# First feed-forward of a two-layer backbone: x times scale into the up-products, the root multiplied in behind them

## The chip, the cores and the metric

The kernel runs on one core of a Trainium2 chip. The metric is the device time of one execution in microseconds; the kernel before has a median of 1995.95 us over 3 runs.

## The reference, cut to what matters

The model has two layers over 512 latent tokens and 256 context tokens with 1024 features. Layer 0 is retention and a gated ConvFFN, layer 1 neighbourhood attention and a gated ConvFFN on the latents. The change is in layer 0, between the retention's output projection and the feed-forward.

```python
def _rmsnorm(x, w):
    y = xf * lax.rsqrt(jnp.mean(xf * xf, axis=-1, keepdims=True) + NORM_EPS)
    return (y * w).astype(x.dtype)

x = x + g1 * y
h2 = _rmsnorm(x, norm2_w) * (1 + sc2) + sh2
x = x + g2 * _conv_ffn(h2, w_up, conv_w, conv_b, w_down)

def _conv_ffn(h, w_up, conv_w, conv_b, w_down):
    u = h @ w_up                       # 1024 -> 2 x 2816
    u = conv over 3 neighbouring tokens, per feature, zeros outside, + conv_b
    a, g = jnp.split(u, 2, axis=-1)
    return (jax.nn.silu(a) * g) @ w_down
```

The scale and the shift are one value per feature and condition (latent, context); the root is one value per token.

## The kernel before, in words

Features lie on the 128 partitions, tokens along the free dimension; x is 8 chunks of 128 features by 768 tokens (512 latent, then 256 context). Each product is done with both operands split in a rounded part (`_hi`) and the rest (`_lo`), as three matmuls: `w_hi` with `h_hi`, `w_hi` with `h_lo`, `w_lo` with `h_hi` (`product`, L404), each once for 512 and once for 256 columns. A block in this document is one chunk of 128 input features in one such product: 6 matmuls. `project` is 8 blocks into one accumulator of two banks; two accumulators take turns, and TensorE waits for `acc_taken` before it opens one again.

Weights come as 512 KB chunks on SP's queue into two `raw` buffers. ScalarE copies each to `w_hi` (L873), VectorE computes `w_lo` (L1304) and counts `lo_split`, which TensorE waits for and which lets SP load the next chunk. There are two slots for split chunks and a spare one.

The order on each engine is the order in the code, with semaphores between engines. In the retention's last output projection (`out_projection`, final) each of 8 tiles m has 4 blocks. VectorE adds it into x (`add_gated`, L1476), ScalarE squares x (L915, the last in two parts, L923 and L925), and VectorE adds the square to `ss` (L1329). Then `final_sums` on TensorE sums over features with matmuls against ones (L480 the sum so far, L488 the last square), ScalarE takes the root (L903), VectorE its reciprocal (L1335), and `spread_roots` brings it to all partitions (L455). TensorE fills the waits with `keep_busy` matmuls (L471). The norm then makes h chunk by chunk: VectorE x times scale times root (L1451), ScalarE plus shift, rounded, into `h_hi` (L955), VectorE the rest into `h_lo` (L1460). `project_two` (L503) does the first two up-products block by block in step with this.

The feed-forward takes its 22 pairs of feature blocks in groups of 8, 8 and 6: for each pair two projects (ups), and after each group 8 tiles down into x. The first two down tiles are interleaved (`outputs_start`, L662), with the last block of each behind the others. For each pair `inner` runs on ScalarE and VectorE: ScalarE evicts the accumulator into `u` (L1074) with pad columns that are zero, VectorE does the three taps (L1665, L1666, L1668), ScalarE Silu (L1080), VectorE the product (L1677), ScalarE `act_hi` (L1085), VectorE `act_lo` (L1685). In between VectorE computes the modulation for layer 1 from rows that POOL's queue loads (`ada_step`, L1416 and L1418): for two conditions in the first group, for one later.

## Time and profile before

| | |
|---|---|
| runs | 1997.66, 1995.95, 1995.14 us |
| profiled execution | 1995.96 us |
| its span | 1993.9 us |
| TensorE matmuls | 1964.6 us busy |
| VectorE | 1288.7 us busy |
| ScalarE | 717.5 us busy |
| GpSimd | 93.0 us busy |

The span is what the profiler records between first and last instruction; the execution's own time lies around it. Times of rows are microseconds from the start of the span unless marked ns. A matmul in plain fp32 (L455, L480, L488) is recorded as two. Some matmul records are missing, so counts can fall short by a few. In a list by line, the columns are line, engine, operation, output<-inputs, shapes and count, then total busy us and mean ns of one, then idle time before. In a list in order of time they are start, duration, engine, line, operation, and in brackets the idle time before and what ended it.

### The profile page before, as it was taken

The page shows a single profiled execution, that of the slowest core. Times are in us where ns is not written, and L with a number is a line of the kernel's source. Part 1 is how long each engine was busy: PE and PEld are TensorE (multiplying, and loading weights), DVE is VectorE, ACT ScalarE, POOL GpSimd, SP SyncE. Part 2 cuts the span into 40 slices and gives each one's busy share as a digit, 9 for nine tenths or more (in the row PEclk, how much of TensorE's full clock was granted, in tenths as well). Part 3 has the DMA queues.
Part 4 walks back from the last instruction along what each step waited for, and adds up shares of the span by engine and source line. Part 5 has one row for each costly group of instructions (what it writes and reads, how often), then busy time and mean ns, then how long its engine had stood idle before and what let it go on. Part 6 is the DMA issues. An engine that isn't in the chain of part 4 may idle for free.

```text
span 1993.9 us, 29041 instructions
## 1 busy us (share of the span) xinstructions
PE 1964.6 (99%) x10628; PEld 1684.8 (84%) x10628; DVE 1288.7 (65%) x1976; ACT 717.5 (36%) x1111; POOL 93.0 (5%) x161
## 2 busy tenths in 40 slices
PE   8999999999999999999999999999999999999998
PEld 8888888888888888888888888788888778888886
DVE  7865645735645677765665467867777777467376
ACT  5433224223313343312331233355665543233243
POOL 0000000000000000000000000211111000000000
PEclk9999999999999999999999999999999999999999
DMA  7321311321222112233223323321111322233223
GB/s 307 99 88 64 106 64 54 106 71 57 85 95 64 54 64 95 95 121 115 94 94 125 116 95 127 121 98 55 53 49 48 106 85 95 95 95 103 86 95 106
DMA packets 51268, 186.56 MB, mean 94 GB/s; under 512 B 5680, under 2 KB 5680, under 8 KB 51184
## 3 DMA queue, kind: packets, MB, share of 16 engines
q1 hardware_dynamic: 37744, 136.73, 20.8%
q0 software_dynamic: 13440, 48.63, 7.4%
q8 instruction: 62, 1.02, 0.2%
q14 instruction: 22, 0.18, 0.0%
HBM read 181.15 MB, written 4.19 MB: 93 GB/s over the span
## 4 chain that ended last, share of the span: by engine, by line
PE 94%; DVE 2%; ACT 1%; DMA 1%; issue 1%; SPq 0%; DVEq 0%; ACTq 0%; POOLq 0%
PE acc L404 60%; PE acc L722 6%; PE o_ps L541 4%; PE acc L662 4%; PE o_ps L572 3%; PE acc L541 3%; PE o_ps L722 2%; PE acc L559 2%; PE acc L503 2%; PE acc L757 1%; PE o_ps L708 1%; PE o_ps L687 1%; PE acc L695 1%; DMA ada_start<-in_ada_first_dram 1%; PE o_ps L455 1%
## 5 line engine op out<-in xcount | busy, mean ns | idle before, releaser
L873 ACT ACTIVATE w_hi<-raw 128x1024 fp32r<-128x1024 f32 x223 | 235.8, 1057 | 582.8 <-PE acc L404 466.8
L404 PE MATMUL acc<-h_hi,w_hi 128*128 128x512 f32 x1520 | 434.2, 349 | 3.5 <-ACT u L1074 1.8
L1304 DVE TENSOR_TENSOR w_lo<-raw,w_hi 128x1024 fp32r<-128x1024 f32 x223 | 272.8, 1223 | 252.4 <-ACT w_hi L873 250.8
L404 PE MATMUL acc<-h_lo,w_hi 128*128 128x512 f32 x1520 | 434.8, 349 | 0.0
L404 PE MATMUL acc<-h_hi,w_lo 128*128 128x512 f32 x1520 | 433.7, 348 | 0.0
L404 PEld LDWEIGHTS acc<-h_hi,w_hi 128*128 128x128 f32 x1520 | 243.6, 188 | 43.4 <-ACT u L1074 2.6
L404 PEld LDWEIGHTS acc<-h_hi,w_lo 128*128 128x128 f32 x1520 | 244.5, 188 | 39.3
L404 PEld LDWEIGHTS acc<-h_lo,w_hi 128*128 128x128 f32 x1520 | 243.6, 188 | 38.2
L1476 DVE SCALAR_TENSOR_TENSOR x<-acc,mod,x 128x512 f32<-128x512 f32 (+3 forms) x137 | 82.0, 634 | 149.5 <-PE acc L404 120.0
L404 PE MATMUL acc<-act_hi,w_hi 128*128 128x512 f32 (+1 forms) x396 | 119.9, 356 | 1.3 <-DVE x L1476 1.3
L404 PE MATMUL acc<-act_hi,w_lo 128*128 128x512 f32 (+1 forms) x396 | 120.2, 357 | 0.0
L404 PE MATMUL acc<-act_lo,w_hi 128*128 128x512 f32 (+1 forms) x396 | 119.5, 355 | 0.0
L1418 DVE CUSTOM_DVE_ANT_0 ada_raw<-ada_raw,silu_rows 128x1024 f32<-128x1024 f32 x80 | 97.8, 1223 | 7.5 <-DMA ada_raw<-in_ada_dram 5.7
L321 POOL DMA_DIRECT2D ada_raw<-in_ada_dram x79 | 41.8, 529 | 1164.7 <-DVE mod_new L1418 1164.7
L1085 ACT ACTIVATE act_hi<-scratch 128x768 f32 (+3 forms) x44 | 32.6, 740 | 141.3 <-DVE scratch L1677 141.3
L1666 DVE SCALAR_TENSOR_TENSOR scratch<-u,taps,scratch 128x769 f32<-128x769 f32 (+1 forms) x88 | 78.1, 887 | 3.1
L1668 DVE SCALAR_TENSOR_TENSOR scratch<-u,taps,scratch 128x769 f32<-128x769 f32 (+1 forms) x88 | 78.0, 887 | 3.1
L404 PEld LDWEIGHTS acc<-act_hi,w_hi 128*128 128x128 f32 x396 | 65.1, 187 | 15.1 <-DVE x L1476 3.5
L404 PEld LDWEIGHTS acc<-act_lo,w_hi 128*128 128x128 f32 x396 | 65.1, 188 | 12.1
L404 PEld LDWEIGHTS acc<-act_hi,w_lo 128*128 128x128 f32 x396 | 65.1, 187 | 11.6
L1074 ACT ACTIVATE u<-acc 128x512 f32<-128x512 f32 (+1 forms) x132 | 62.9, 514 | 24.5 <-PE acc L404 24.5
L1172 ACT ACTIVATE pt_hi<-acc 128x512 fp32r<-128x512 f32 x64 | 38.3, 599 | 84.2 <-PE acc L695 84.1
(263 smaller groups left out, 3385.3 us busy)
## 6 DMA issues: line engine op xcount, KB each, us to landing
raw<-in_weights_dram SPq DMA_DIRECT2D x232, 512.0 KB, 3.4
ada_raw<-in_ada_dram POOLq DMA_DIRECT2D x80, 512.0 KB, 3.8
ada_start<-in_ada_first_dram SPq DMA_DIRECT2D x8, 1024.0 KB, 19.9
x<-in_x_in_dram SPq DMA_DIRECT2D x4, 768.0 KB, 7.4
park_dram<-x POOLq DMA_DIRECT2D x1, 2048.0 KB, 8.1
rel<-in_bias_dram POOLq DMA_DIRECT2D x16, 128.0 KB, 2.4
x<-park_dram POOLq DMA_DIRECT2D x2, 1024.0 KB, 6.6
out_dram<-x SPq DMA_DIRECT2D x8, 256.0 KB, 2.2
```

The lines of the kernel that those rows point to most:

```text
L404: mm = nc.tensor.matmul(tile[:, c0:c0 + cn], wt[:, b * P:(b + 1) * P], mv[:, n, c0:c0 + cn], start=(n == 0 and m == 0), stop=(n == last an ...
L541: mm = nc.tensor.matmul(tile, hs[:, k, t * P:(t + 1) * P], ws[:, d * RV:(d + 1) * RV], start=(k == 0 and m == 0), stop=(last and m == 2))
L572: mm = nc.tensor.matmul(tile, vt[:, c0:c0 + P], pt[i % 2][:, p0:p0 + qn], start=((context or i == 0) and n == 0 and m == 0), stop=(i >= 5 ...
L662: mm = nc.tensor.matmul(tile[:, c0:c0 + cn], wt[:, n * P:(n + 1) * P], mv[:, n, c0:c0 + cn], start=(n == 0 and m == 0), stop=(n == size - ...
L722: mm = nc.tensor.matmul(tile[:, c0:c0 + cn], wt[:, n * P:(n + 1) * P], mv[:, n, c0:c0 + cn], start=(n == 0 and m == 0), stop=(n == KC - 1 ...
L873: nc.scalar.activation(w_hi[i][:, :] if spare is None else spare[0], raw[r][:, :], ACT.Copy).then_inc(hi_split, 1)
L1074: ins = nc.scalar.activation(u[j][:, c0 + c + 1:c0 + c + 1 + cn], tile[:, c0:c0 + cn], ACT.Copy)
L1304: nc.vector.tensor_tensor(lo, raw[r][:, :], hi.bitcast(F32), ALU.subtract).then_inc(lo_split, 1)
L1418: nc.vector.tensor_tensor_reduce(ada_raw[:, :], ada_raw[:, :], silu_rows[:, 0, :], 1.0, 0.0, ALU.mult, ALU.add, mod_new[:, j, 0:1]).then_i ...
L1476: ins = nc.vector.scalar_tensor_tensor(xv, tile[:, c0:c0 + cn], mod[:, layer, bass.ds(gate + m, 1), c:c + 1].rearrange("p a c -> p (a c)") ...
L1666: step(nc.vector.scalar_tensor_tensor(S[j][:, 0:width], u[j][:, 1:1 + width], tap(1), S[j][:, 0:width], ALU.mult, ALU.add))
L1668: nc.vector.scalar_tensor_tensor(S[j][:, 0:width], u[j][:, 2:2 + width], tap(2), S[j][:, 0:width], ALU.mult, ALU.add).then_inc(conv_done, 1)
```

## The change

The scale is made before the output projection (`lift_scale`). As each chunk of x is complete, ScalarE and VectorE write x times scale, without the root and the shift, into `h_hi` and `h_lo` (`scaled_hi`, `scaled_lo`). Two columns behind the 768 hold the shift for the latents and for the context, so the row of `h_hi` and `h_lo` is 770 long and the second matmul of each up-product has 258 columns (`WITH_SHIFT`). The norm and the double product are gone in this place; two ordinary projects stand there, and the sums of squares (`sums_so_far`, `last_sums`, the two halves of `final_sums`) and `spread_roots` stand before blocks 3, 4 and 6 of the first. ScalarE copies the spread roots into `ss`. VectorE, and no longer ScalarE, evicts each up-product, times `ss`, into `u`. The shift's product is constant along the tokens: it goes times the sum of the taps into the bias (`lifted`), and the pads of `u` hold its negative; each part now has pads of its own. The first tap is done by ScalarE and no longer by VectorE. Layer 1 keeps its order. `lift` now shares its place with `cond`, and POOL's two waits on `norm_t` count 8 less, for the norm that is gone.

```diff
-        h_hi = sb("h_hi", [P, KC, TOK], F32R)
-        h_lo = sb("h_lo", [P, KC, TOK], F32R)
+        h_hi = sb("h_hi", [P, KC, TOK + 2], F32R)
+        h_lo = sb("h_lo", [P, KC, TOK + 2], F32R)
...
+                def ready_and_chain(n):
+                    ready(n)
+                    if n in chain:
+                        chain[n]()
...
+                        if chain is None:
+                            project_two(ups, ready, spare)
+                        else:
+                            project(h_hi, h_lo, ups, ready_and_chain)
+                            project(h_hi, h_lo, ups, None, spare)
...
             out_projection(True)
-            final_sums(TOK)
-            keep_busy(2)
-            spread_roots(PARTS, True)
-            keep_busy(12)
-            ffn(PARTS, spare1)
+            ffn(WITH_SHIFT, PARTS, spare1, {3: lambda: sums_so_far(TOK), 4: lambda: last_sums(TOK), 6: lambda: spread_roots(PARTS)})
...
+            def scaled_hi(k):
+                for c0, cn, c in PARTS:
+                    ins = nc.scalar.activation(h_hi[:, k, c0:c0 + cn], x[:, k, c0:c0 + cn], ACT.Identity, scale=norm_a[:, k, c:c + 1])
+                ins.then_inc(h_hi_done, 1)
+            def copy_spread():
+                root(D, TOK, True)
+                act.wait_ge(spread_done, roots.now())
+                nc.scalar.activation(ss[:, :], spread[:, 0:TOK], ACT.Copy).then_inc(spread_copied, 1)
...
                         if j < splits:
                             split()
-                        if j == 0:
-                            act.wait_ge(conv_done, convs.now() + (layer + 1))
-                        for c0, cn, c in parts:
-                            ins = nc.scalar.activation(u[j][:, c0 + c + 1:c0 + c + 1 + cn], tile[:, c0:c0 + cn], ACT.Copy)
-                        ins.then_inc(acc_taken[i], 1)
+                        if layer:
+                            if j == 0:
+                                act.wait_ge(conv_done, convs.now() + 1)
+                            nc.scalar.activation(u[j][:, 1:1 + LAT], tile[:, 0:LAT], ACT.Copy).then_inc(acc_taken[i], 1)
+                        else:
+                            act.wait_ge(acc_taken[i], after)
+                            for c0, c1, c in ((0, LAT + 2, 0), (LAT + 2, TOK + 2, 1)):
+                                ins = nc.scalar.activation(S[j][:, c0:c1], u[j][:, c0:c1], ACT.Identity,
+                                                           scale=taps[:, 4 * j:4 * j + 1], bias=lifted[:, j, c:c + 1])
+                            ins.then_inc(conv_begun, 1)
                         if spare is not None and j == 0:
                             split(spare)
-                    act.wait_ge(conv_done, convs.now() + (layer + 2))
...
                         last_square(t, after, TOK)
                     else:
                         final_square(t, after, 2 * c, m, TOK)
+                    if c == 0 and m == 0:
+                        act.wait_ge(scale_made, 1)
+                        nc.scalar.activation(h_hi[:, :, TOK:TOK + 2], mod[:, 0, 24:24 + KC, :], ACT.Copy)
+                    scaled_hi(2 * c + m)
                     if c == OUT_SLOTS - 1 and m == 0:
                         split(spare1)
-            x_final()
-            norm(0, 24, PARTS)
+            copy_spread()
             ffn(0, PARTS, False)
...
+            def scaled_lo(k):
+                dve.wait_ge(h_hi_done, h_hi_made.up())
+                for c0, cn, c in PARTS:
+                    ins = nc.vector.scalar_tensor_tensor(h_lo[:, k, c0:c0 + cn], x[:, k, c0:c0 + cn], norm_a[:, k, c:c + 1],
+                                                         h_hi[:, k, c0:c0 + cn].bitcast(F32), ALU.mult, ALU.subtract)
+                ins.then_inc(h_lo_done, 1)
...
             def out_projection(with_ada, first_ada=0, final=False):
                 if final:
                     step(nc.vector.memset(ss[:, :], 0.0))
+                    lift_scale(0, 2, 24, 2).then_inc(scale_made, 1)
                 own_done()
                 for m in range(KC):
                     add_gated(m, 0, 16, PARTS, final and m == KC - 1)
...
                     if final and m < KC - 1:
                         add_square(m % 2, TOK)
+                    if final:
+                        scaled_lo(m)
+                    if final and m == 0:
+                        nc.vector.tensor_tensor(h_lo[:, :, TOK:TOK + 2], mod[:, 0, 24:24 + KC, :],
+                                                h_hi[:, :, TOK:TOK + 2].bitcast(F32), ALU.subtract)
                     if final and m == KC - 2:
                         split(spare1)
...
                 if final:
                     squares_made.up()
+                    h_split.up(KC)
+                    one_over(TOK)
+                    dve.wait_ge(spread_copied, 2)
...
                     conds = 2 if n == 0 else 1
                     ups = UP_ADA[n] if with_ada else 0
                     steps = [(hi_splits, 2), (own_steps, 5 + ups * conds), (silus, 1), (act_hi_made, 1)]
-                    steps += [(ada_loads, 16 * ups), (ada_made, ups)]
+                    steps += [(ada_loads, 16 * ups), (ada_made, ups), (begun, 0 if layer else 2)]
                     def inner(f, splits, spare=None):
-                        step(nc.vector.tensor_copy(taps[:, :], conv[:, layer, bass.ds(f + f0, 1), :].rearrange("p a c -> p (a c)")))
+                        step(nc.vector.tensor_copy(taps[:, 0:8], conv[:, layer, bass.ds(f + f0, 1), :].rearrange("p a c -> p (a c)")))
+                        if not layer:
+                            own = lambda t: taps[:, 0:8].rearrange("p (j t) -> p t j", t=4)[:, t, :]
+                            step(nc.vector.tensor_tensor(taps[:, 8:10], own(0), own(1), ALU.add))
+                            step(nc.vector.tensor_tensor(taps[:, 8:10], taps[:, 8:10], own(2), ALU.add))
                         for j in range(2):
                             i, _, _, after = A.next()
                             dve.wait_ge(acc_full, A.full.now())
+                            tap = lambda t: taps[:, 4 * j + t:4 * j + t + 1]
+                            if not layer:
+                                tile = acc[i]
+                                nc.vector.scalar_tensor_tensor(lifted[:, j, :], tile[:, TOK:TOK + 2], taps[:, 8 + j:9 + j],
+                                                               tap(3).to_broadcast([P, 2]), ALU.mult, ALU.add)
+                                for c, ends in ((0, slice(0, LAT + 2, LAT + 1)), (1, slice(LAT + 2, TOK + 4, CTX + 1))):
+                                    nc.vector.tensor_scalar(u[j][:, ends], tile[:, TOK + c:TOK + c + 1].to_broadcast([P, 2]), -1.0, None,
+                                                            ALU.mult)
+                                for c0, cn, c in parts:
+                                    at = c0 + 2 * c + 1
+                                    ins = nc.vector.tensor_tensor(u[j][:, at:at + cn], tile[:, c0:c0 + cn], ss[:, c0:c0 + cn], ALU.mult)
+                                ins.then_inc(acc_taken[i], 1)
                             if j < splits:
                                 split()
-                            dve.wait_ge(acc_taken[i], after)
-                            tap = lambda t: taps[:, 4 * j + t:4 * j + t + 1]
-                            step(nc.vector.tensor_scalar(S[j][:, 0:width], u[j][:, 0:width], tap(0), tap(3), ALU.mult, ALU.add))
+                            if layer:
+                                dve.wait_ge(acc_taken[i], after)
+                                step(nc.vector.tensor_scalar(S[j][:, 0:width], u[j][:, 0:width], tap(0), tap(3), ALU.mult, ALU.add))
+                            else:
+                                dve.wait_ge(conv_begun, begun.up())
                             step(nc.vector.scalar_tensor_tensor(S[j][:, 0:width], u[j][:, 1:1 + width], tap(1), S[j][:, 0:width],
...
                         for c0, cn, c in parts:
-                            ins = nc.vector.tensor_tensor(S[3][:, c0:c0 + cn], S[2][:, c0 + c:c0 + c + cn],
-                                                          S[1][:, c0 + c:c0 + c + cn], ALU.mult)
+                            own = slice(c0 + 2 * c, c0 + 2 * c + cn)
+                            ins = nc.vector.tensor_tensor(S[3][:, c0:c0 + cn], S[2][:, own], S[1][:, own], ALU.mult)
...
             out_projection(0, final=True)
-            pads()
-            norm(0, 2, 24, PARTS, False)
             ffn(0, PARTS, True, False)
```

## Rows read from the trace of the kernel before

**Rows 1.** The page: engines, and the chain that ended last by engine.
```profile
PE 1964.6 (99%) x10628; PEld 1684.8 (84%) x10628; DVE 1288.7 (65%) x1976; ACT 717.5 (36%) x1111; POOL 93.0 (5%) x161
...
PE 94%; DVE 2%; ACT 1%; DMA 1%; issue 1%; SPq 0%; DVEq 0%; ACTq 0%; POOLq 0%
```

**Rows 2.** The chain in order of time: start, duration, what; longest pieces.
```profile
677.83 25.48 PE acc L404 x144
...
712.40 16.76 PE acc L503 x90
...
731.05 118.99 PE acc L404 x672
850.04 15.72 PE acc L662 x90
...
866.98 183.79 PE acc L404 x1056
```

**Rows 3.** The chain again, 665 to 765 us, with its short pieces.
```profile
703.31 1.28 PE o_ps L480 x12
...
705.58 1.30 PE o_ps L488 x12
...
707.51 1.17 PE o_ps L455 x8
...
729.18 1.06 ACT w_hi L873
730.24 0.77 ACT u L1074 x2
```

**Rows 4.** Busy by engine in stretches: length, PE, PEld, DVE, ACT, POOL, PEclk, DMA.
```profile
703.30:712.40 9.10, 8.45 (x56) 7.02 (x54) 6.20 (x19) 4.50 (x10) 0.00 (x0) 1.00 0.35 115
...
731.00:850.00 119.00, 118.95 (x673) 103.13 (x674) 91.50 (x126) 37.07 (x63) 3.70 (x7) 1.00 0.29 95
```

**Rows 5.** In order of time, 690 to 735 us: one chunk of the norm.
```profile
713.34 1.14 DVE L1460 SCALAR_TENSOR_TENSOR h_lo<-scratch,mod,h_hi 128x512 fp32r<-128x512 f32 x2
713.46 1.13 ACT L955 ACTIVATE h_hi<-scratch,mod 128x512 fp32r<-128x512 f32 x2 [1.41 <-DVE scratch L1451]
```

**Rows 6.** In order of time, 665 to 700 us: the first tiles' adds.
```profile
676.54 1.14 DVE L1476 SCALAR_TENSOR_TENSOR x<-acc,mod,x 128x512 f32<-128x512 f32 x2 [0.75 <-PE acc L618]
...
677.77 0.84 ACT L915 ACTIVATE scratch<-x 128x768 f32<-128x768 f32 x1 [3.77 <-DVE x L1476]
...
678.65 0.96 DVE L1329 TENSOR_TENSOR ss<-ss,scratch 128x768 f32<-128x768 f32 x1 [0.96 <-ACT scratch L915]
...
679.52 1.14 DVE L1476 SCALAR_TENSOR_TENSOR x<-acc,mod,x 128x512 f32<-128x512 f32 x2
```

**Rows 7.** ScalarE in order of time, 703 to 760 us.
```profile
702.18 1.28 ACT L896 ACT_TABLE_LOAD   x1
...
703.59 1.04 ACT L873 ACTIVATE w_hi<-raw 128x1024 fp32r<-128x1024 f32 x1
704.54 0.61 ACT L923 ACTIVATE scratch<-x 128x512 f32<-128x512 f32 x1
```

**Rows 8.** VectorE by line and shape, 15 to 90 us.
```profile
L1533 DVE TENSOR_TENSOR vg_lo<-acc,vg_hi 128x512 fp32r<-128x512 f32 x4 | 2.6, 686 | 3.1 <-ACT vg_hi L983 3.1
...
L1356 DVE TENSOR_SCALAR norm_a<-mod_new,lift,small 128x2 f32<-128x2 f32 x8 | 2.3, 288 | 0.3
...
L1515 DVE TENSOR_TENSOR qk_lo<-acc,qk_hi 128x256 fp32r<-128x256 f32 x1 | 0.4, 425 | 0.0
```

**Rows 9.** VectorE by line and shape, 660 to 850 us.
```profile
L1665 DVE TENSOR_SCALAR scratch<-u,taps 128x769 f32<-128x769 f32 x15 | 10.2, 678 | 0.0
```

**Rows 10.** ScalarE in order of time, 0 to 30 us.
```profile
25.86 1.31 ACT L939 ACTIVATE scratch<-scratch,mod,norm_a 128x512 f32<-128x512 f32 x2 [1.10 <-DVE scratch L1373]
```

**Rows 11.** VectorE in order of time, 800 to 870 us.
```profile
856.10 0.95 DVE L1685 TENSOR_TENSOR act_lo<-scratch,act_hi 128x768 fp32r<-128x768 f32 x1
```

**Rows 12.** The page: one of the costliest groups.
```profile
L404 PE MATMUL acc<-h_hi,w_hi 128*128 128x512 f32 x1520 | 434.2, 349 | 3.5 <-ACT u L1074 1.8
```

More of the change, by code:

```diff
@@ L61 @@
 PARTS = ((0, LAT, 0), (LAT, CTX, 1))
+WITH_SHIFT = ((0, LAT, 0), (LAT, CTX + 2, 1))
 WIDE = 64
@@ L203, in backbone @@
                 u = [sb(f"u{i}", [P, TOK + 4], stack=part) for i in range(2)]
-                taps = sb("taps", [P, 8], stack=part)
+                taps = sb("taps", [P, 10], stack=part)
+                lifted = sb("lifted", [P, 2, 2], stack=part)
                 waste = sb("waste", [P, D], stack=part)
@@ L406, in product, with project @@
                 mm.then_inc(acc_full, 1)
-            def project(hi, lo, parts, ready=None):
-                w = next_chunk()
+            def project(hi, lo, parts, ready=None, spare=None):
+                w = next_chunk(spare)
                 product(open_acc(), w, range(KC), hi, lo, parts, ready)
@@ L471, in keep_busy, with sums_so_far @@
                     nc.tensor.matmul(o_ps[:, 2, :] if place is None else place, w[:, 0:P], w[:, 0:LAT], start=True, stop=True)
-            def final_sums(width, ends=False):
-                if not ends:
-                    pe.wait_ge(lo_split, chunk.now() + 1)
-                half = LAT if width == TOK else LAT // 2
+            def sums_so_far(width):
                 pe.wait_ge(sq_added, squares_added.up(KC) - 1)
@@ L490, in final_sums @@
                 mm.then_inc(sums_done, 1)
+            def final_sums(width, ends=False):
+                if not ends:
+                    pe.wait_ge(lo_split, chunk.now() + 1)
+                sums_so_far(width)
+                keep_busy(4)
+                last_sums(width)
             def project_two(parts, ready, spare, tiles=None):
@@ L626, in out_projection, with ffn @@
                         product(open_acc(), w, range(m * VC, (m + 1) * VC), hi, lo, PARTS)
-            def ffn(parts, spare):
+            def ffn(ups, downs, spare, chain=None):
                 ready = h_ready(h_split.now())
                 first = True
+                def ready_and_chain(n):
+                    ready(n)
+                    if n in chain:
+                        chain[n]()
                 for size in GROUPS:
@@ L638, in ffn @@
                         h_split.up(KC)
-                        project_two(parts, ready, spare)
+                        if chain is None:
[3 more added lines that the diff above has]
+                            project(h_hi, h_lo, ups, None, spare)
                     with turns(pe, size - first, A.steps(2) + [(chunk, 2)]):
-                        project(h_hi, h_lo, parts)
-                        project(h_hi, h_lo, parts)
+                        project(h_hi, h_lo, ups)
+                        project(h_hi, h_lo, ups)
                     first = False
                     act_split.up(size)
-                    outputs_start(size, parts, act_ready, spare)
+                    outputs_start(size, downs, act_ready, spare)
                     with turns(pe, 3, A.steps(2) + [(chunk, 2)]):
@@ L648, in ffn @@
                             w = next_chunk()
-                            product(open_acc(), w, range(size), act_hi, act_lo, parts)
+                            product(open_acc(), w, range(size), act_hi, act_lo, downs)
             def outputs_start(size, parts, ready, spare):
@@ L1432, in norm @@
                 own_done()
-                step(nc.vector.scalar_tensor_tensor(
-                    norm_a[:, :, 0:n], mod[:, layer, shift + KC:shift + 2 * KC, 0:n], 1.0,
-                    norm_w[:, which, :].rearrange("p (k c) -> p k c", c=1).to_broadcast([P, KC, n]), ALU.add, ALU.mult))
+                step(lift_scale(layer, which, shift, n))
                 one_over(width)
@@ L1481, in add_gated, with lift_scale @@
                 ins.then_inc(acc_taken[i], 1)
+            def lift_scale(layer, which, shift, n):
+                return nc.vector.scalar_tensor_tensor(
+                    norm_a[:, :, 0:n], mod[:, layer, shift + KC:shift + 2 * KC, 0:n], 1.0,
+                    norm_w[:, which, :].rearrange("p (k c) -> p k c", c=1).to_broadcast([P, KC, n]), ALU.add, ALU.mult)
+            def scaled_lo(k):
[4 more added lines that the diff above has]
+                ins.then_inc(h_lo_done, 1)
             def out_projection(with_ada, first_ada=0, final=False):
```

33 lines of the change are left out of this document (19 added, 14 removed).

## The prediction

> **What bounds the kernel now.** I read the engine shares first, then the chain that ended last, and then went closer only where the change works. TensorE is busy 99% of the span and makes up 94% of the chain [rows 1]: time is won only where TensorE stands idle or does work that nothing needs. The chain shows one such place in reach: out-projection tiles run from 677.83 for 25.48 us, the double first product of the feed-forward starts only at 712.40, and the plain run of up-products only at 731.05 [rows 2]. Between them stand the norm (sums of squares 1.28 and 1.30, spread of the roots 1.17, the rest waiting for ScalarE and VectorE) and, after the double product, a gap in which a weight split (1.06) and an eviction (0.77) come first [rows 3]. So 703.31 to 731.05, 27.74 us, is the stretch to watch. The granted clock there is 1.00, the 2.4 GHz level [rows 4]; it is not what costs.
>
> **A block of product.** A project is 8 blocks of 6 matmuls. 14 projects took 118.99 us for 672 matmuls: 0.1771 us each, 1.06 us a block, 8.50 a project. The later ups and downs took 183.79 for 1056, that is 0.1740 each or 1.04 to 1.05 a block [rows 2]. Out-projection tiles have 4 blocks: 25.2 us for 6 tiles, 4.20 each.
>
> **Part 1: the stretch.** Taken out of it: the wait for roots, the first scaled h, and the waiting gap at its end. Left on TensorE: 16 blocks at 1.06 = 16.96 us, plus the three small groups now between the blocks: 1.28 + 1.30 and, for the whole spread of which the chain shows the first 8 of 12 matmuls (1.17), 1.3. Sum 20.8 us. Against 27.74 this frees 6.9 us if nothing waits. Now what waits:
>
> **Part 2: out-projection on ScalarE and VectorE.** Per tile ScalarE adds scaled_hi (like L955, 1.13 us for the two parts) and VectorE scaled_lo (like L1460, 1.14) [rows 5]. VectorE works in order: the add of tile m at G, ScalarE's square from G+1.23 to G+2.07 [rows 6], scaled_hi to about G+3.1, VectorE's add of the square from G+2.1, scaled_lo from G+3.15, next add at G+4.2. The weight split of the odd tiles falls into the wait for the square. The cycle is thus 4.2 us, just the 4.20 of a tile: VectorE keeps pace but has no reserve. It starts late: behind tile 0 stand scaled_lo(0), the two shift columns and their ScalarE copy (about 0.1 to 0.2 each on either engine, like other operations on a few columns), so the add of tile 1 moves from 679.52 [rows 6] to 681.0. It frees its accumulator at 682.1, and TensorE, done with tile 2 at 682.03, waits 0.25 us. Each later add ends within 0.05 us of TensorE's need. Cost: 0.25 us; lower bound 0; upper bound, if each of six cycles runs as much over as the first, 6 x 0.25 = 1.5.
>
> **Part 3: the last tile.** Add 6 starts at 702.0 and TensorE starts the first project at 703.56. ScalarE then does square 6, scaled_hi(6), the split into the spare (from 705.0), the table load (1.28) and its dummy, a split (1.04), and only then the half squares [rows 7]. With the same spacing they come at 708.5 to 709.4 and scaled_hi(7) ends at 710.4, so scaled_lo(7) ends at 711.6. TensorE: blocks 0 to 2 end at 706.7, sums so far at 708.0, block 3 at 709.1, and the half square is there at 709.2. The wait for it has all further blocks queued behind it; I take 0.1 us, bounds 0 and 2 (ScalarE's list half as long again). The reciprocal, behind scaled_lo(7) on VectorE, is ready at 711.7 and the spread is asked for at 712.6, after block 5: hidden with 0.9 us to spare. Block 7 needs scaled_lo(7): hidden by 3 us. The accumulator is full at 716.1; ScalarE's copy of the spread (0.8) is done at 715.1 and its Silu table (1.28) loads beside the eviction. The second project runs to 724.7, the first tile is taken near 717.7, so the third project starts without a wait at 724.7 and not at 731.05. **Gain 6.35 us.** The weight loads on SP's queue follow the splits that move later by about 5 us, and land long before the split at 716; no DMA is added. POOL's waits get smaller counts for the same later event: nothing.
>
> **Part 4: the up loop.** VectorE was busy 91.50 of 119 us, 13.1 us for each of 7 pairs (a pair of projects, one pass of the loop, is 16.96) [rows 4]. Taken out: two first taps of 0.68 [rows 9]. Added twice: the eviction (0.69 + 0.43, 1.03 with overlap, [rows 8]), the lifted columns (0.29, [rows 8]) and two pads of 0.1 to 0.2; once: two sums of taps. 13.1 - 1.4 + 2.1 + 1.1 + 0.4 = 15.3 us of 16.96. ScalarE swaps an eviction for a tap with two pointer operands (1.31 for both parts, [rows 10]). The added wait is VectorE's for that tap: in it 1.3 us pass while VectorE has 1.14 us of split to do; behind it stand the other taps, the ada step and the next eviction. Following the order through, a pair needs about 16.6 us in the first group and 1.2 less later, where the ada step has one condition. TensorE waits only when an eviction comes some 6 us late, or the last act_lo: before it ended 7.0 us after the last project of a group [rows 2, 11], now about 8.2; it is wanted after 10 blocks, 10.5 us, in the group of six and after 14 elsewhere. Cost 0, hidden by the other tile's project; upper bound 1 us a pair over pace, of which the 6 us of reserve swallow all but 1 us in the first group.
>
> **Part 5: two columns.** 352 blocks have 3 matmuls that grow from 256 to 258 columns, 1056 in all. 2 columns at 2.4 GHz are 0.83 ns: 0.9 us. Unknown is how TensorE takes 258 columns and rows of h at 770 instead of 768 elements; no row shows either. The nearest rows are the blocks themselves, which run at 1.04 to 1.06 us without a cause that I can see: bounds -0.02 us on the first group's 112 blocks (-2.2 us) and +0.02 on the 224 of the later groups (+4.5), which with the 0.9 gives -1.3 and +5.4. I take 0.9, since the columns are the only known change.
>
> The Trainium skill (VectorE: DVE Perf Modes, the section on the TRN2 errata) prices a matmul at 6 cycles plus its columns. By it a pair of 512 and 256 would take 0.325 us, where the rows give 0.348 to 0.354, so the measured time decides for the fixed part; for two more columns the rule gives 0.83 ns too, and the estimate for this part would stay 0.9 us. What it speaks against is any step in the cost above 256 columns.
>
> **Sum.** 1995.96 us (the profiled execution; span 1993.9 and 2.1 around it; the median of the runs is 0.01 away) - 6.35 + 0.9 = 1990.5. With the 0.2 us on the middle of part 2's and 3's bounds I say **1990.7**.
>
> **Rivals.**
> A, the in-order chain. VectorE has no reserve in the out-projection; if each cycle is 4.45 us and the last square comes late, 1.5 + 1.0 us are lost: 1993.2. For it: 4.2 against 4.20. Against it: the split's overlap was seen in the rows, and the first project needs only six finished blocks at once.
> B, the slower side: rows of h at a stride of 3080 bytes. If this holds TensorE up, it does so in every product with h, in the retention and the second layer as well. 1520 matmuls of one kind [rows 12], less 336 in the second layer's ups, are 592 two-part blocks; at +0.02 us each 11.8 us: 2002.5. From 0.009 us a block on, all gain is gone. For it: blocks of equal work do differ by 0.02 us. Against it: the slow ones and the fast ones share the same stride now.
> C, the first group's blocks fall from 1.06 to 1.04: 2.2 us more gain, 1988.5. For it: every later group does so [rows 2]. Against it: the same instructions kept 1.06 for 119 us.
> D, VectorE sets the pace of the up loop, as the work moved onto it is slower than planned (1 us over pace in all 7, 8 and 6 pairs, of which the reserve swallows 6 us a group): 1, 2 and 0 us, and act_lo of the last group 3.7 us late: 1997.4. For it: 15.3 of 16.96 us. Against it: the adds all come from rows of like shape.
>
> **Chances.** Forecast 0.52 (own range 1989.2 to 1992.2), A 0.15, B 0.13, C 0.13, D 0.07. Faster by over 0.2% (4.0 us, about what a measurement of this kernel can tell from no change) means below 1992.0: 0.48 of the forecast, C, a little of A: 0.62. Slower by that much: most of B and a bit of D, 0.10. The rest 0.28. The range, 1987.8 to 1998, takes in C, A, D and a mild B.
>
> **What would show it.** Right: in the chain no norm between the out-projection and the up-products; the first up-product within 0.5 us of 703.5; sums and spread between its blocks; the third project near 724.7; VectorE 15 to 15.5 us busy a pair, with TensorE never waiting for an eviction. Wrong: TensorE waiting on x or on the half square over 1 us (A); blocks with h over 1.07 us, also in the retention (B); a wait on evictions or act_lo in the loop (D).

## The result: 0.5% slower

The changed kernel takes 2004.57 us (median of 5 runs, 2003.50 to 2005.77) against 1995.14 (1994.28 to 1997.66) for the kernel before (5 runs): a ratio of 1.0046, 95% interval 1.0035 to 1.0056. Forecast was 1990.7, with 1987.8 to 1998.0 as range. The profiled execution took 2004.57, its span 2002.7 (1993.9 before).

The page of the changed kernel, engines and chain; they answer to [rows 1]:
```profile
PE 1975.4 (99%) x10610; PEld 1688.9 (84%) x10610; DVE 1313.2 (66%) x2173; ACT 741.8 (37%) x1113; POOL 93.2 (5%) x161
...
PE 94%; DVE 2%; DMA 1%; ACT 1%; issue 1%; SPq 0%; DVEq 0%; POOLq 0%; ACTq 0%
```
TensorE has 18 matmul records fewer and is busy 10.8 us longer, at a granted clock of 0.998 (0.997 before). So the loss lies in the matmuls themselves, neither in a wait nor in the clock. The chain says where (start, duration, what):
```profile
70.21 42.29 PE acc L406 x240
...
157.31 81.53 PE acc L406 x462
...
682.43 28.95 PE acc L406 x162
...
718.58 129.84 PE acc L406 x732
848.41 15.83 PE acc L682 x90
865.47 187.46 PE acc L406 x1056
1052.93 15.83 PE acc L682 x90
1069.98 152.70 PE acc L406 x864
1222.68 11.61 PE acc L682 x66
...
1620.90 10.97 PE acc L513 x45
1633.49 78.30 PE acc L406 x336
...
1723.01 122.43 PE acc L406 x528
```
and of the kernel before, the rows of the same view that stand in no group above:
```profile
71.25 42.39 PE acc L404 x240
...
158.33 80.41 PE acc L404 x462
...
1067.73 150.51 PE acc L404 x864
1218.24 11.56 PE acc L662 x66
...
1615.59 10.95 PE acc L503 x45
1628.15 76.46 PE acc L404 x336
...
1715.96 120.95 PE acc L404 x528
```
Take the difference of the starts (after less before) at equal pieces: -1.04 us near 71, +4.60 where the out-projection begins (682.43 against 677.83), -1.63 at the end of the first group's ups (848.41, 850.04), +2.16 before the next downs, +4.44 at 1222, +5.31 at 1620, +8.8 at the end. So the changed stretch and its loop gained 6.23 us, as the prediction wanted, while the retention up to there, whose instructions the change leaves alone, lost 5.64, the later groups 3.79 and 2.28, the attention 0.87 and the second layer 3.49. Equal pieces show it without sums: 462 matmuls 81.53 for 80.41, 336 of the second layer 78.30 for 76.46.

The stretch itself, the chain in short pieces:
```profile
711.38 1.29 PE o_ps L479 x12
712.67 1.11 PE acc L406 x6
713.78 1.28 PE o_ps L490 x12
715.06 2.18 PE acc L406 x12
717.24 1.34 PE o_ps L457 x12
```
Sums, half sums and spread stand between blocks with nothing in between, and behind them 732 matmuls run in one piece: the wait for the roots and the gap of [rows 3] are gone.

### The profile page after: what moved, and what is told of

Read it like the earlier page. It is cut to its first block, busy times and chain, and to the rows that moved or that the text cites. A ratio compares the mean times of both kernels' runs of the same rounds, so it can differ in the third digit from the quotient of the medians.

```text
span 2002.7 us, 29213 instructions
## 1 busy us (share of the span) xinstructions
PE 1975.4 (99%) x10610; PEld 1688.9 (84%) x10610; DVE 1313.2 (66%) x2173; ACT 741.8 (37%) x1113; POOL 93.2 (5%) x161
## 4 chain that ended last, share of the span: by engine, by line
PE 94%; DVE 2%; DMA 1%; ACT 1%; issue 1%; SPq 0%; DVEq 0%; POOLq 0%; ACTq 0%
PE acc L406 62%; PE acc L742 6%; PE o_ps L551 4%; PE acc L682 4%; PE o_ps L582 3%; PE acc L551 3%; PE o_ps L742 2%; PE acc L569 2%; PE acc L777 1%; PE o_ps L728 1%; PE o_ps L707 1%; PE acc L715 1%; PE acc L513 1%; DMA ada_start<-in_ada_first_dram 1%; PE o_ps L457 1%
## 5 line engine op out<-in xcount | busy, mean ns | idle before, releaser
L406 PE MATMUL acc<-h_hi,w_hi 128*128 128x512 f32 (+2 forms) x1536 | 443.0, 352 | 2.6 <-issue 1.7
L406 PE MATMUL acc<-h_lo,w_hi 128*128 128x512 f32 (+2 forms) x1536 | 442.7, 351 | 0.0
L406 PE MATMUL acc<-h_hi,w_lo 128*128 128x512 f32 (+2 forms) x1536 | 441.9, 351 | 0.0
L1342 DVE TENSOR_TENSOR w_lo<-raw,w_hi 128x1024 fp32r<-128x1024 f32 x223 | 272.5, 1222 | 188.7 <-ACT w_hi L889 187.4
L406 PEld LDWEIGHTS acc<-h_hi,w_hi 128*128 128x128 f32 x1536 | 248.6, 189 | 44.8 <-issue 2.3
L406 PEld LDWEIGHTS acc<-h_lo,w_hi 128*128 128x128 f32 x1536 | 248.6, 189 | 42.2
L1744 DVE SCALAR_TENSOR_TENSOR scratch<-u,taps,scratch 128x770 f32<-128x770 f32 (+1 forms) x88 | 78.0, 887 | 17.4 <-ACT scratch L1108 15.9
L1746 DVE SCALAR_TENSOR_TENSOR scratch<-u,taps,scratch 128x770 f32<-128x770 f32 (+1 forms) x88 | 78.0, 887 | 3.1
L1108 ACT ACTIVATE scratch<-u,lifted,taps 128x514 f32<-128x514 f32 x88 | 57.9, 706 | 46.0 <-DVE u L1735 46.0
L406 PEld LDWEIGHTS acc<-act_lo,w_hi 128*128 128x128 f32 x396 | 65.0, 188 | 10.8
```

Source lines behind the costliest of these rows:

```text
L406: mm = nc.tensor.matmul(tile[:, c0:c0 + cn], wt[:, b * P:(b + 1) * P], mv[:, n, c0:c0 + cn], start=(n == 0 and m == 0), stop=(n == last an ...
L1108: ins = nc.scalar.activation(S[j][:, c0:c1], u[j][:, c0:c1], ACT.Identity, scale=taps[:, 4 * j:4 * j + 1], bias=lifted[:, j, c:c + 1])
L1342: nc.vector.tensor_tensor(lo, raw[r][:, :], hi.bitcast(F32), ALU.subtract).then_inc(lo_split, 1)
L1744: step(nc.vector.scalar_tensor_tensor(S[j][:, 0:width], u[j][:, 1:1 + width], tap(1), S[j][:, 0:width], ALU.mult, ALU.add))
L1746: nc.vector.scalar_tensor_tensor(S[j][:, 0:width], u[j][:, 2:2 + width], tap(2), S[j][:, 0:width], ALU.mult, ALU.add).then_inc(conv_done, 1)
```

## The experiments

The question: what slows matmuls that are the same instructions as before? What differs for them is the memory. Rows of h are 3080 bytes long instead of 3072, and behind the two longer tensors everything moved: h_lo by 64 bytes, the weights by 128, all tensors of the stages by 96; among these are vg, the moving operand (the one streamed past the weights) of the output projection, and act, that of the downs. The layout theory says that row length and places alone cost the time. The first rival, mix, says that the added work of VectorE and ScalarE gets in TensorE's way; the second, columns, that the two columns cost far more than 0.83 ns. (The expectations call the layout M in e1, its two halves S, the row length, and B, the places, in e2 and e3, and both rivals together P.) Each ratio is to the kernel before in runs beside it. A piece below is a stretch of the chain.

**e1_layout**: the program before, with the changed kernel's memory (`lift` in the place of `cond` too).
```diff
-        h_hi = sb("h_hi", [P, KC, TOK], F32R)
-        h_lo = sb("h_lo", [P, KC, TOK], F32R)
+        h_hi = sb("h_hi", [P, KC, TOK + 2], F32R)
+        h_lo = sb("h_lo", [P, KC, TOK + 2], F32R)
```


> The program of before with the memory layout of after and nothing else of the change: rows of h_hi and h_lo of 770 elements, lift in the place of cond, so that all tensors behind h lie where after has them. Theory M (memory layout: the stride of h, or the places of the tensors behind it, slows the matmuls): the retention loses the 5.4 us that it lost in after (add of tile 0 at about 681), the later stages some 9 more, 2007 to 2011 us in all. Theory P (the loss belongs to the changed program, its 258 columns or its work on VectorE): 1995 to 1997, add of tile 0 at 676 to 677.

2010.21 us, 1.0070 (1.0053 to 1.0086). The chain of this kernel:
```profile
157.55 81.53 PE acc L403 x462
...
871.73 186.49 PE acc L403 x1056
...
1639.51 78.30 PE acc L403 x336
```
81.53 and 78.30 to the hundredth as in the changed kernel. The layout alone costs 14 us, more than the whole loss; in this layout the change's own work gains about 6 (the span is 2008.8 here, 2002.7 with the change).

**e2_places**: rows of 768 as before, but all tensors where the change put them (64 unused bytes behind h_hi and behind h_lo).

> The program of before, rows of h at 768 elements as before, but 64 bytes left free behind h_hi and behind h_lo and lift in the place of cond: every tensor lies where after has it, only the stride of h is that of before. If the stride alone slows (theory S): 1995 to 1998 us, output projection tiles at 4.20 us. If the places do it (theory B: a start off 64 bytes for the retention's and feed-forward's own tensors): as the first kernel, 2005 us and more, output projection tiles at 4.24 us, since those read no h at all.

2000.92, 1.0028 (1.0018 to 1.0039), between the two forecasts. The places cost about 5 us, the row length, on top of them, the other 9.

**e3_rows784**: the changed program; the changed feed-forward has rows of its own, 784 elements, laid over h and dist; everything else lies at its old remainder.
```diff
+            g_hi = sb("g_hi", [P, KC, ROW], F32R, part)
+            g_lo = sb("g_lo", [P, KC, ROW], F32R, part)
```


> The program of after with h at 768 elements a row everywhere but in the changed feed-forward, which has views of its own with rows of 784 elements (3136 bytes, a multiple of 64) over h and dist; lift as before, so that the tensors behind lie at the same remainder of 64 as before. Theories S and B: the retention is back to the times of before, the gain of the changed stretch stays (6.2 us from the add of tile 0 to the end of the first group's ups) and the total is 1988 to 1991 us. Theory P: no better than 2002.

1992.30, 0.9981 (0.9972 to 0.9991): faster than before, and just above the 1988 to 1991 forecast. Retention and second layer are back (80.41, 76.46); the ups of the later groups still take 186.34 and 152.42 us.

**e4_256cols**: the changed kernel with 256 columns in the second matmul; the product of the shift is left out.
```diff
-WITH_SHIFT = ((0, LAT, 0), (LAT, CTX + 2, 1))
+WITH_SHIFT = PARTS
```


> The program and layout of after with 256 instead of 258 columns in the second matmul of each up-product (the product of the shift is left out, so the output is another). If two columns cost what columns cost: 0.9 us less than after, 2003.7. If 258 crosses a step: 3 to 5 us less, 2000 to 2001.5, with blocks of 1.04 in the groups of 8 and 6. If only the layout matters: 2003 to 2004.

2002.84, 1.0034 (1.0022 to 1.0047). The three up pieces took 129.05, 186.50 and 152.66 us, 1.8 us less than with 258 columns; here the columns explain no more than that.

**e5_784_256cols**, **e6_768_256cols**, **e7_rows800**: e3_rows784 with 256 columns; with 256 columns and rows of 768 (in both the shift's product is left out, in the second its two copies too); with rows of 800 and all of the change.

> The version with rows of 784 for the changed feed-forward, its second matmul of 256 columns instead of 258, so that the product of the shift is left out. Question: in the version with 258 columns the stretches that hold the ups of the second and third group still took 186.3 and 152.4 us against 183.8 and 150.5 in the kernel before. If the two columns cost it: 183.8 and 150.5 come back and the time is about 1988. If the length of the rows costs it (784 as 770): 186 and 152 stay, about 1991.5, the two columns being worth 1 us. If it is the other mix of work on VectorE and ScalarE: the same as for the rows, and the version with rows of 768 tells the two apart.

> The same, with rows of 768 as everywhere before, so without room for the shift columns: neither their two small copies nor their product are made. All else of the change is in. If the row length holds TensorE up: 183.8 and 150.5 us in the two stretches and 1986 to 1988 us, 8 to 10 below the kernel before. If the other mix of work on VectorE and ScalarE slows TensorE in the up loop: 186 and 152 stay and about 1991.

> The version with 784-element rows, with 800 instead (3200 bytes, a multiple of 128 where 3136 is only one of 64), shift and 258 columns in. If only a multiple of 64 counts: as with 784, 1992.3 within 1 us, 186.3 and 152.4 in the two stretches. If a larger power of two counts: below 1991, with 184 to 185.5 and 151 to 152. If what counts is how far 8 rows lie apart in the memory, not their remainder: slower than 784, 1993 to 1994.

e5 1990.13, 0.9972 (0.9962 to 0.9982); e6 1987.15, 0.9961 (0.9947 to 0.9976); e7 1992.81, 0.9985 (0.9975 to 0.9995). The three up pieces took 128.50, 185.50 and 151.78 us in e5 and 126.89, 183.81 and 150.53 in e6. But for the two small copies, all of VectorE's and ScalarE's new work is in e6, and TensorE takes 183.81 and 150.53 us where it took 183.79 and 150.51 before: the mix has fallen. By these pieces rows of 784 cost 4.6 us against 768 (by the medians 3.0). In e7, with 800, the pieces are those of e3 (129.32, 186.35, 152.43).

**e8_starts**: the kernel before with 32 unused bytes ahead of h_hi and 32 ahead of ss.

> The kernel before with 32 free bytes ahead of h_hi and 32 ahead of ss, and nothing else: h, raw and the weights move from a remainder of 32 to 0 by 64, and all other tensors keep theirs (x too). If a start off a multiple of 64 slows TensorE whatever the tensor, the kernel before pays for it in h and the weights: 5 to 10 us faster, about 1987 to 1991. If starts only count against each other (two tensors read at once want different remainders): slower, 2000 or more. If only the tensors of the stages count: 1996, the same.

2002.04, 1.0028 (1.0016 to 1.0041), a miss: h and weights at a multiple of 64 are no better. The piece of 183.79 rose to 186.50, that of 150.51 to 152.59 and the retention's projects of 48 matmuls from 8.32 to 8.48, while the first group (118.98) and the second layer (76.45) kept their time. A rule by absolute starts doesn't give that.

**m1_places** and **m2_map** measure the disputed cost by itself: TensorE alone runs blocks of six, each case with other places, rows or columns; no part of the reference is computed. Each is one run.

> The disputed cost by itself: a kernel that computes nothing of the reference, only blocks of six matmuls as in a project (8 blocks to a project, 2 projects to a pass, 3 passes, so 48 blocks a case), each case with other places of h_hi, h_lo and the weights or another row length, between marks of six small matmuls. VectorE, ScalarE and the DMA queues stand still in the first 26 cases and VectorE and ScalarE are busy in the last 5. If TensorE's own reads set the pace: the places of the kernel before take 49.9 us a case (1.04 a block), those of the changed kernel 51.1 (1.065), rows of 784 with 258 columns 50.9, and a single moved tensor shows which place it is. If it is contention with the other engines: all of the first 26 take the same for the same columns, and only the last 5 differ. If neither: all 31 are alike, and the loops of the kernel itself (waits, where their code lies) are to be looked at.

> 91 cases of 16 blocks each by TensorE alone (nothing of the reference is computed), to find by what the block's time goes. In the case with the places of the kernel before, h_hi, h_lo and the weights all start at the same remainder by 1024 bytes (160) and a block took 1.06; h_lo 128 bytes further or h 32 bytes further took 1.04. If what counts is how the two operands of one moment lie to each other (moving rows against the weights that are loaded beside them): the same for equal differences, whatever the absolute start, periodic in the difference, and 1.04 wherever the difference is far enough from 0. If the absolute start counts: moving all three together by 32 changes it, moves of one by 256 or 512 do not. If the accumulator counts (which of the two goes with which half of the weights): the cases with the other order differ, which would explain why the same places take 1.06 in the first group of the kernel before and 1.04 in the later ones. Expected for 16 blocks: 16.64 to 17.1 us, in steps of 0.107. Two more columns: 0.04 us a case if they cost 0.83 ns a matmul, 0.11 and more if in steps.

In m1 the places of the kernel before took 50.88 us for 48 blocks in the repeated case, those of the changed kernel 51.12, h 32 bytes further alone 49.93. The expectation had 49.9 for the first of these, a miss: taken alone, the old places are slow too. The chain of m1, in order the changed kernel's places, the same with 256 columns, those of e2, the old ones repeated:
```profile
91.51 51.12 PE acc L117 x288
...
143.34 50.74 PE acc L117 x288
...
194.79 50.25 PE acc L117 x288
...
1271.81 50.88 PE acc L117 x288
```
With 256 columns the changed kernel's places took 50.74 and those of e2 50.25, less than the old ones. Per block 51.12, 50.74 and 50.25 are 1.065, 1.057 and 1.047; in the first group of the changed kernel, of e4 and of e2 a block took 1.064, 1.058 and 1.049. So the cases give the time of the new places in the whole kernel. Only places with all differences at 0, the old ones and those of e6, have two values: the old ones take 1.06 in the cases and in the first group of the kernel before, but 1.04 in its retention and in the ups of its later groups. What the layout cost in blocks of six is mostly that 1.04: a retention project of 48 matmuls went from 8.32 to 8.46, that is from 1.040 to 1.057 a block. Blocks of three went from 0.683 to 0.699 in the second layer (76.46 and 78.30 by 112), and in the cases likewise from 0.681 to 0.697 (32.67 and 33.44 by 48).

With VectorE and ScalarE busy, five cases (in the last VectorE and ScalarE stopped early) gave the same as without within 0.01, but for the very first case of the run. DMA queues stood still. So the times come with TensorE's own operands. In m2 a case is 16 blocks; rows of the chain:
```profile
58.48 16.95 PE acc L91 x96
...
146.22 16.64 PE acc L91 x96
...
356.89 16.64 PE acc L91 x96
...
426.65 16.96 PE acc L91 x96
...
619.79 16.86 PE acc L91 x96
...
1059.96 16.86 PE acc L91 x96
...
1236.03 16.93 PE acc L91 x96
...
1271.35 16.66 PE acc L91 x96
1288.71 10.90 PE acc L91 x48
1300.31 11.20 PE acc L91 x48
...
1464.78 16.64 PE acc L91 x96
```
In order: the places before; h 32 bytes further; h_lo 128 further; h_lo 256 further; weights 128 further; rows of 784; 258 columns at the places before; 258 columns with h 32 further; then blocks of three (512 columns only) at the places before and with h 32 further; last, rows of 832, h 32 further. Divided by 16, by the difference of two starts modulo 256 bytes (us a block; the other difference 0):
```
difference                  0      32     64     96     128    160    192    224
weights less h_hi           1.060  1.059  1.059  1.041  1.054  1.050  1.060  1.041
h_lo less h_hi              1.060  1.053  1.047  1.047  1.040  1.040  1.054  1.047
weights less h, three alone 0.681                       0.700  0.701  0.687  0.700
```
Moving h instead of the weights gives the same as moving the weights the other way (within 0.002); moving one by 256 or 512, or all three by 32, changes nothing. The very first case of the run took 17.63 us, and 16.96 when repeated as the last; it is left out. Rows of 832 or 1024 elements, multiples of 256 bytes, keep a block at one value; rows of 770, 776, 784 or 800 let the blocks wander over the table: 784 took 1.054 where 768 could have 1.040. The table holds for 256 columns. With 258 a block at the places before took 1.058 and with h 32 further 1.041, within 0.002 of 256, but with h_lo 128 further 1.060 where 256 columns took 1.040. So two columns have no one price. The order of the accumulators does not matter.

**e10_weights_224** puts the table to the test in the kernel before: 224 bytes of small tensors go from behind the weights to ahead of them, nothing else.
```diff
         h_lo = sb("h_lo", [P, KC, TOK], F32R)
+        norm_a = sb("norm_a", [P, KC, 2])
+        silu_c = sb("silu_c", [P, KC, 2])
+        mod_new = sb("mod_new", [P, 8, 2])
+        rms = sb("rms", [P, 8])
```


> The kernel before with four small tensors (224 bytes) taken from behind the weights to ahead of them and nothing else: the weights and raw move by 224 bytes, h and the tensors of the stages keep their places. Difference of the starts, weights less h, by 256: 0 before, 224 now; weights less activations 160 before, 128 now. By the map: blocks of six with h at 1.04 in all stages, so the first group's ups fall from 118.99 to about 116.6 and 8.32 for a project of 48 stays; blocks of three (512 columns alone) with h in the second layer rise from 0.681 to 0.700, so 76.46 to about 78.4 and 120.95 to 122 to 123; in sum 1996 to 2000. If the map of the separate kernel does not carry over: 1996 with no such pattern.

2002.20, 1.0029 (1.0017 to 1.0041); the chain:
```profile
731.12 116.75 PE acc L404 x672
...
864.80 183.97 PE acc L404 x1056
...
1628.17 78.66 PE acc L404 x336
...
1718.17 123.34 PE acc L404 x528
```
Both opposite movements came, 116.75 (forecast 116.6) and 78.66 (78.4), from moving the weights by 224 bytes. The total missed its forecast of 1996 to 2000: the stretch from the third group's downs through the attention (1216.36 to 1615.60 us) lost another 1.9 us, which the forecast from the table did not have.

**e9_rows832**, **e11_832_acts_64**: e3_rows784 with rows of 832 (near is taken under the rows as well), without and with 64 unused bytes ahead of the tensors of the stages.

> The changed program with rows of 832 elements (3328 bytes, 13 times 256) for the changed feed-forward, 258 columns, everything else placed as in the kernel before. In the map of cases only the differences of the starts by 256 bytes counted, and rows of a multiple of 256 bytes kept a block at one value. So the three up stretches should come back: 129.3 to about 127, 186.3 to about 184, 152.4 to about 151 us, and the time to 1986 to 1988, 4 to 6 below the version with rows of 784. If the two columns cost their 2.2 ns a matmul at any row length: 1989. If rows of 784 were not what held it up: 1992, as before.

> The version with rows of 832 and 64 free bytes ahead of the tensors of the stages, so that weights less activations is 96 by 256 instead of 160. By the map a block of six with act or vg falls from 1.05 to 1.04: 176 blocks of downs and 128 of the out-projection at 0.01, 3 us below the version without the free bytes, about 1984. Blocks of three with the activations of the second layer were not in the map at 96; 176 of them could change by up to 0.02 us either way. Rival: the first group's and the retention's h blocks take the slower of two values seen at the same places (8.32 to 8.48 and 183.8 to 186.5), as when the stage tensors were moved by 64 together with h: then 1988 to 1992.

e9 1993.01, 0.9983 (0.9974 to 0.9992), a miss: 129.32, 186.36 and 152.44, just as with 784. The expectation overlooked that with 258 columns a difference of 0 stands at 1.06 in the table's cases: steady, but steadily slow. That does not explain all of it: e6, with 256 columns and the same difference of 0, ran at 1.04. e11 1991.44, 0.9972 (0.9963 to 0.9982), where 1984 or, by the rival, 1988 to 1992 was forecast: 0.5 us off each long piece with downs, but 0.15 added to every other 48-matmul project of the retention (8.47 for 8.32).

**e12_832_g_32**, **e13_832_g_32_acts**: e9 and e11 with one more line, which starts the rows 32 bytes further, so that weights less h is 224 there and 0 elsewhere.
```diff
+            sb("ahead_g", [P, 8], stack=part)
             g_hi = sb("g_hi", [P, KC, ROW], F32R, part)
```


> The version with rows of 832, its rows of the changed feed-forward begun 32 bytes further, so that weights less h is 224 by 256 bytes there and 0 in all other stages as before. In the map blocks of 256 + 2 columns at this difference took 1.041 and at 0 1.058 to 1.06. If the difference of the starts is what is left: the three up stretches fall from 129.3, 186.4 and 152.4 to about 127.2, 184.2 and 150.9, and the time by 5.8 us, to about 1987. If the two columns cost as measured before (2.2 ns a matmul) whatever the places: 1990 to 1991. If the stretches stay: 1993.

> The same with the 64 free bytes ahead of the tensors of the stages. These took 0.5 us off each of the two long stretches with downs and 0.2 off the out-projection, and cost 0.15 in each head's first project: 1986, 1 us below the version without them. If the two changes disturb each other: 1988 or more.

e12 1985.78, 0.9947 (0.9933 to 0.9960); e13 1985.35, 0.9942 (0.9928 to 0.9955), alike within the intervals. The chain of e12:
```profile
712.05 126.88 PE acc L412 x732
...
855.95 183.84 PE acc L412 x1056
...
1056.81 150.53 PE acc L412 x864
...
1617.28 76.45 PE acc L412 x336
```
32 bytes took 7.2 us off e9, as forecast (about 1987). With 258 columns and the whole change, these pieces are those of e6 with 256 columns, 126.89 and 183.81: at this start the two columns cost nothing that can be read, as in m2 (16.66 for 16.64). It is the version that beats both kernels, by 10.6 us (0.5%) and, over the two comparisons, by some 19 (0.9947 against 1.0046).

## Why the prediction was wrong

- **What bounds it**: right. Nothing but TensorE is on the chain, and it is just for that reason that 0.02 us a block counts 1:1.
- **Parts 1 and 3, the stretch**: right. Forecast -6.35, measured -6.23 with blocks of 1.064. From the start of the out-projection on (4.60 us later than before) the first project came at 682.43 + 28.95 - 3 x 1.06 = 708.2, forecast 703.56 + 4.60 = 708.16. The half squares were done at 713.6 and their sums began at 713.78, straight behind the block; the spread was asked for at 717.24 (forecast 717.2). The three groups took 3.91, forecast 3.88.
- **Part 2**: right in the order and the cycle, and close in the sum partly by luck. VectorE in order of time in the changed kernel:
```profile
681.15 1.14 DVE L1513 SCALAR_TENSOR_TENSOR x<-acc,mod,x 128x512 f32<-128x512 f32 x2 [0.52 <-PE acc L628]
...
685.53 1.14 DVE L1513 SCALAR_TENSOR_TENSOR x<-acc,mod,x 128x512 f32<-128x512 f32 x2
```
 The first cycle is 4.38 us (forecast 4.46), the next 4.13 to 4.18; TensorE lost 0.3 (708.2 less 703.31 and 4.60), forecast 0.25. But the layout alone, without the new work, made the 144 matmuls of six tiles 25.67 us long (e1_layout) instead of 25.48, so the wait that was forecast is only about 0.1 of the 0.3. Rival A did not come.
- **Part 4**: right in the cost, too high in VectorE's work. Busy by engine in the up loop (length, PE, PEld, DVE, ACT, POOL, PEclk, DMA), the whole of it and six pairs, and six pairs before:
```profile
718.60:848.40 129.80, 129.80 (x733) 113.33 (x733) 104.14 (x203) 49.49 (x69) 3.72 (x7) 1.00 0.27 87
...
735.00:837.12 102.12, 102.12 (x577) 89.16 (x576) 83.09 (x163) 38.60 (x54) 3.19 (x6) 1.00 0.28 93
...
735.00:837.00 102.00, 102.00 (x579) 88.43 (x578) 77.13 (x108) 31.95 (x55) 3.70 (x7) 1.00 0.28 93
```
 VectorE has 83.09 / 6 = 13.8 us a pair and had 12.9: 1.0 more, where the sum added 2.2 to 13.1. Its sign, 15 to 15.5, did not come; that TensorE never waits did. The last act_lo ends at 855.44 + 0.95, 8.0 us after the last up-product (forecast 8.2). Rival D did not come.
- **Part 5 is the step that failed**: "I take 0.9, since the columns are the only known change". They were not: the row length and the places of all tensors behind h were changed too. In the changed kernel weights less h is 128, h_lo less h_hi 64 and weights less act or vg 192 modulo 256 bytes, where it was 0, 0 and 160, and rows are no multiple of 256. By e1_layout this costs 14 us (e2: 5 for the places, the rest for the rows). The term was taken at 0.9 and the layout at nothing. The bounds, -1.3 to +5.4, covered only the products of the changed feed-forward; the loss lay in products with h, act and vg all over the kernel, in both layers (a few pieces got faster, the second layer's L682 10.30 for 10.41). The two columns themselves cost 2.2 ns a matmul in rows of 784 (the three up pieces of e3 less those of e5, 2.3 us over some 1040) and nothing that can be read at the best start (e12). The Trainium skill (VectorE: DVE Perf Modes, TRN2 errata) prices two columns at 0.83 ns, between these two; no run here shows that price.
- **Rival B**, rows of h at 3080 bytes, was nearest: right in that products with h pay in the retention and the second layer too, and that the row length costs (9 of the 14 us, e1 less e2, against its 11.8). It did not have the places (5 us), nor that products with vg and act pay. That its 2002.5 came so near 2004.6 is luck, as these two errors partly cancel; its sign, blocks over 1.07, did not come (1.057 in the retention, 1.064 in the ups). It was given 0.13 because "the slow ones and the fast ones share the same stride". That was the clue read the wrong way: equal strides with 1.04 and 1.06 showed that something beside the stride sets the block's time, and the change moved that too.
- **Rival C** did not come in the changed kernel, whose first group ran at 1.064. It came in other layouts: in e6 and e12 the first group's blocks take 126.9 / 122 = 1.04 us. With them the change is worth 9.3 us on this stretch (676.03 to 838.93 in e12, 162.90 us, against 172.21), not 6.35.

What is shown and what is not: that the layout cost the time is shown by e1_layout, and that better places give it back by e12. What stays open is the mechanism below that. At a difference of 0 the same places give 1.06 in one stage of the kernel before and 1.04 in others, and 1.06 in the cases. e8_starts moved the retention's projects and the later groups from one value to the other though h, h_lo and the weights moved together, and e11 every other project though only tensors of the stages moved. So there are two rhythms there, and what picks one was not found. At 224, with rows of 768, 832 or 1024, only 1.04 was seen in blocks of six. Why 256 bytes is the period is not known.

## What to carry to other kernels

Before forecasting a change on a kernel that TensorE bounds, list what it does to addresses: a row that grows by 8 bytes changes every matmul that reads it and moves every tensor behind it. Count its cost over all matmuls of the kernel, not over those of the changed stage. Rows of moving operands at multiples of 256 bytes kept a block's time in one place, but by themselves won nothing (e9 took as long as e3 with 784); only together with the start did they (e12). When memory has moved, measure the old program in the new layout first: that one run told the mechanism's gain and the layout's loss apart.

## What the runs showed of the hardware

TensorE's fp32r blocks of six (three of 512 columns, three of 256), in rows of 768, ran in m2 at 1.040 to 1.060 us and blocks of three (512) at 0.681 to 0.701, by the difference of the starts of weights and moving rows modulo 256 bytes; the best place for the one is not the best for the other (224: 1.041 and 0.700; 0: 1.060 and 0.681). Neither figure is a price for a whole kernel: at a difference of 0 stages of the kernel before ran at 1.04 too. VectorE and ScalarE running beside TensorE changed no case of m1 by more than 0.01 us in 50; DMA traffic was not tried there. The Trainium skill (SBUF — State Buffer, Operand start alignment) asks only for a start at a multiple of the element size, and its runs timed nothing; every start here fulfils that, and the blocks still took 1.040 to 1.060 us by their starts.
